# Stage boundaries by token tile: what a reordered normalisation and a new buffer layout do in a two-block transformer kernel

## The reference

```python
def rms_norm(x, g):
    xf = x.astype(jnp.float32)
    y = xf * lax.rsqrt(jnp.mean(xf * xf, -1, keepdims=True) + EPS)
    return (y * g.astype(jnp.float32)).astype(x.dtype)

for i in range(DEPTH):                       # DEPTH = 2
    a = rms_norm(h, norm_g[i, 0])
    a = mixer(a, ...)                        # i = 0: latent attention, i = 1: differential attention
    h = h + rms_norm(a, norm_g[i, 1])
    f = conv_ffn(rms_norm(h, norm_g[i, 2]), ffn_w_up[i], ffn_conv_w[i], ffn_conv_b[i], ffn_w_down[i])
    h = h + rms_norm(f, norm_g[i, 3])
# hybrid layer: rms_norm(h, g_mix) @ w_in, attention, then 32 experts, of which each token takes 2
```

## Time and profile before

| what | us |
|---|---|
| three runs | 1342.06, 1345.78, 1347.07; median 1345.78 |
| the profiled execution | 1344.84, of which the span from first to last instruction 1343.0 |
| TensorE busy | 1282.2 (95%) |
| GpSimd, ScalarE, VectorE busy | 573.2, 548.2, 509.6 |
| boundary `x1`: first idle-filling matmul to first product | 120.47 to 132.46 |
| boundary `x2` | 316.03 to 328.01 |
| boundary `x3` | 451.98 to 463.96 |
| boundary `x4` | 647.02 to 656.96 |

### The profile page before, as it was taken

The page is one execution under the profiler, slowest core; times in us unless marked ns, Lnnn a source line. Parts: engine busy times, 40 slices in busy tenths (PEclk is TensorE's granted clock), DMA queues, the critical chain, the costliest instruction groups (busy, mean ns, idle before and its releaser), DMA issues.

```text
span 1343.0 us, 20033 instructions
## 1 busy us (share of the span) xinstructions
PE 1282.2 (95%) x7959; PEld 953.8 (71%) x7959; DVE 509.6 (38%) x1303; ACT 548.2 (41%) x853; POOL 573.2 (43%) x136
## 2 busy tenths in 40 slices
PE   6998999999998899999999999999999999999996
PEld 6867999998986799999878888854444444454442
DVE  2434444445265454444657453421111111111112
ACT  4654555556477465555543664311111111111112
POOL 4722788885944188888567855200000000000001
PEclk9999999999999999999999999999999999999998
DMA  7731566664633276664446544889999999999994
GB/s 270 235 94 63 184 194 188 188 193 151 220 126 95 63 205 195 196 188 165 150 164 204 158 137 161 335 342 405 427 428 427 429 429 429 429 428 428 428 424 185
DMA packets 157078, 341.22 MB, mean 254 GB/s; under 512 B 8554, under 2 KB 119499, under 8 KB 144331
## 3 DMA queue, kind: packets, MB, share of 16 engines
q1 hardware_dynamic: 157002, 340.18, 68.2%
HBM read 339.10 MB, written 1.05 MB: 253 GB/s over the span
## 4 chain that ended last, share of the span: by engine, by line
PE 77%; DMA 11%; ACT 4%; DVE 4%; POOL 2%; issue 1%; SPq 0%; ACTq 0%; DVEq 0%
PE bank L683 16%; PE bank L685 15%; PE bank L684 15%; PE bank L1258 12%; DMA ring<-in_w 6%; PE bank L1286 6%; DMA xspare<-in_w 4%; PE bank L1201 3%; PE bank L782 2%; POOL parts L635 2%; PE bank L693 1%; PE bank L1231 1%; ACT parts L1330 1%; PE bank L1119 1%; PE bank L1135 1%
## 5 line engine op out<-in xcount | busy, mean ns | idle before, releaser
L635 POOL TENSOR_TENSOR parts<-raw,parts 128x2048 fp32r<-128x2048 f32 (+4 forms) x128 | 568.0, 4464 | 289.8 <-ACT parts L1330 289.8
L683 PE MATMUL bank<-xh,parts 128*128 128x256 f32 x1032 | 288.0, 279 | 5.8 <-POOL parts L635 3.8
L684 PE MATMUL bank<-xl,parts 128*128 128x256 f32 x1032 | 285.8, 277 | 0.0
L685 PE MATMUL bank<-xh,parts 128*128 128x256 f32 x1032 | 285.8, 277 | 0.0
L1330 ACT ACTIVATE parts<-raw 128x2048 fp32r<-128x2048 f32 (+4 forms) x128 | 236.0, 1852 | 23.4 <-PE bank L683 8.5
L1258 PE MATMUL bank<-ring,room 128*64 128x512 f32 x768 | 226.1, 594 | 7.2 <-DMA ring<-in_w 5.3
L658 POOL TENSOR_TENSOR xn<-h,gpost 128x512 f32<-128x512 f32 x4 | 4.9, 1268 | 474.6 <-DVE h L2283 474.6
L683 PEld LDWEIGHTS bank<-xh,parts 128*128 128x128 f32 x1032 | 193.8, 188 | 12.4 <-issue 4.7
L684 PEld LDWEIGHTS bank<-xl,parts 128*128 128x128 f32 x1032 | 194.0, 188 | 0.8
L685 PEld LDWEIGHTS bank<-xh,parts 128*128 128x128 f32 x1032 | 194.0, 188 | 0.0
L1258 PEld LDWEIGHTS bank<-ring,room 128*64 128x64 f32 x768 | 72.6, 137 | 111.7 <-issue 111.7
(11 more groups left out here) (256 smaller groups left out, 1858.5 us busy)
## 6 DMA issues: line engine op xcount, KB each, us to landing
ring<-in_w SPq DMA_DIRECT2D x67, 2048.0 KB, 22.6
raw<-in_ffn_w_up SPq DMA_DIRECT2D x88, 512.0 KB, 4.9
raw<-in_ffn_w_down SPq DMA_DIRECT2D x44, 512.0 KB, 3.9
room<-in_w SPq DMA_DIRECT2D x11, 2048.0 KB, 19.9
xspare<-in_w SPq DMA_DIRECT2D x11, 2048.0 KB, 25.6
raw<-in_w_in SPq DMA_DIRECT2D x40, 512.0 KB, 4.0
raw<-in_diff_w_qkv SPq DMA_DIRECT2D x24, 512.0 KB, 4.6
ring<-in_w SPq DMA_DIRECT2D x10, 1024.0 KB, 25.0
```

The source lines that it names most:

```text
L635: pool.tensor_tensor(low[:, p % PARTS, 0:n], raw[:, p % RING, 0:n], high[:, p % PARTS, 0:n], ALU.subtract).then_inc(low_ready, 1)
L683: first = pe.matmul(out_, a[0], b[0], start=start, stop=False)
L684: pe.matmul(out_, a[0], b[1], start=False, stop=False)
L685: return first, pe.matmul(out_, a[1], b[0], start=False, stop=stop)
```

## The change

**Steps 2 and 3 go by token tile.** `turned_over` replaces `post`: gains, sums, guess, root and residual of tile 0 are issued before tile 1's, each root as a chain of one-column operations (`half_of`, `root_of`) with a guess of its own. `h` of tile 0 is thus written before tile 1's gain. In a network's last `down`, TensorE now ends the two banks of tile 0 before it does tile 1's.

**Steps 4 and 5 in `x1` to `x3`.** The normalised `xn` is not written any more. For each tile, VectorE makes a diagonal matrix of the roots (`spread_roots`: identity times the root's column, [128 x 128] into `score`), and TensorE multiplies `h` by it (`h_transposed`), which turns and scales in one matmul. A bank now holds two whole feature tiles of [128 x 256], and so all four banks end with tile 1. The gain, which now lies along the partitions, is applied while copying out: `high_chunks` and `low_chunks`, eight operations of [128 x 256] on each engine, with a [128 x 1] column of `gcol` as scale.

**In `x4`** `h` itself is transposed as soon as each tile is there, and the gain is applied in the same way. The sum of squares, the guess and the roots come after.

**`k_tile`** waits bank by bank, at `k` = 0, 2, 4, 6, where there was one wait before the product and one at `k` = 4.

**Matmuls without use:** 23 for 32 in `x1` to `x3`; in `x4` 5, and 11 between the two tiles.

**Gains:** the four rows of gains come by small transfers into the rows that are transposed once in the first mixer, and VectorE copies 32 columns from there to `gcol`. SyncE's loads of `gpre` for these four boundaries are gone.

**Layout:** `xh`, `xl` (with `xspare`), `hh`, `hl`, `h`, `xn`, `room`, `gpre`, `gpost`, `score`, `selT` and `cs` now follow the ring in this order, the small buffers last. By the allocator each of the named ones lies 128 bytes past a multiple of 512, as the ring and `parts` do and did.

```diff
         ring = sb("ring", [P, 3 * RING, HALF])
+        with nc.sbuf_tensor("xh", [P, KT, S], F32R) as xh, nc.sbuf_tensor("xl", [P, KT, S], F32R) as xl:
+            pass
+        xspare = sb("xspare", [P, 2 * HALF])
+        hh, hl = sb("hh", [P, 4, S], F32R), sb("hl", [P, 4, S], F32R)
+        h = sb("h", [P, NT, D])
+        xn = sb("xn", [P, NT, D])
+        room = sb("room", [P, 11648])
+        gpre, gpost = sb("gpre", [P, D]), sb("gpost", [P, D])
+        score = sb("score", [P, NT, S])
+        selT = sb("selT", [P, 2, NT, P], F32R)
...
+            for x, src in enumerate((A["norm_g"][0, 2], A["norm_g"][1, 0], A["norm_g"][1, 2], A["g_mix_2"][0])):
+                rows_on(prow[1 + KT * x:1 + KT * x + KT, 4, :], src)
...
+            def h_transposed(name, site, scaled, between=0):
+                b = [begin(G[name] + q) for q in range(4)]
+                for t in range(NT):
+                    if t and between:
+                        keep_clock(between, bank[4])
+                    if scaled:
+                        pe.wait_ge(spread_ready, 2 * (site - 1) + t + 1)
+                    else:
+                        pe.wait_ge(h_ready, 2 * (site - 1) + t + 1)
+                    for k in range(KT):
+                        at = S * (k % 2) + P * t
+                        dst, src = b[k // 2][:, at:at + P], h[:, t, P * k:P * k + P]
+                        if scaled:
+                            ins = pe.matmul(dst, src, spread_r[:, t], start=True, stop=True)
+                        else:
+                            ins = pe.transpose(dst, src, ident)
+                        if t == 0 and k == 0:
+                            behind(ins)
+                        if t and k % 2:
+                            end(ins, G[name] + k // 2)
+                late.extend([(2 * q, G[name] + q) for q in range(4)])
...
-            WAIT = 32
+            WAIT = 23
             late = []
             def k_tile(k):
-                if k == 4:
-                    while late:
-                        moved(pe, late.pop(0))
+                while late and late[0][0] <= k:
+                    moved(pe, late.pop(0)[1])
...
-                    for x in range(2):
-                        pe.wait_ge(hid_ready, n + (n0 + 1 + x))
-                        for t in range(NT):
-                            for hf in range(2):
-                                first, ins = product(bank[4 + 2 * t + hf][:, :],
-                                                     [y[:, (j + x) % 4, t * P:t * P + P] for y in (hh, hl)],
-                                                     [y[:, x, 512 * hf:512 * hf + 512] for y in w],
-                                                     start and x == 0, stop and x == 1)
-                                behind(first)
-                                if stop and x == 1:
-                                    ins.then_inc(ffn_full, 1)
+                    each = [(x, t, hf) for x in range(2) for t in range(NT) for hf in range(2)]
+                    if stop:
+                        each = [(x, t, hf) for t in range(NT) for x in range(2) for hf in range(2)]
+                    for i, (x, t, hf) in enumerate(each):
+                        if not any(x == y for y, _, _ in each[:i]):
+                            pe.wait_ge(hid_ready, n + (n0 + 1 + x))
+                        first, ins = product(bank[4 + 2 * t + hf][:, :],
+                                             [y[:, (j + x) % 4, t * P:t * P + P] for y in (hh, hl)],
+                                             [y[:, x, 512 * hf:512 * hf + 512] for y in w],
+                                             start and x == 0, stop and x == 1)
+                        behind(first)
+                        if stop and x == 1:
...
+            keep_clock(WAIT // 4, bank[3])
+            h_transposed("x4", 4, False, WAIT // 2)
...
+            def high_chunks(name, site):
+                for k in range(KT):
+                    g = G[name] + k // 2
+                    full(act, g)
+                    act.activation(xh[:, k, :], bank[BANK[g]][:, S * (k % 2):S * (k % 2) + S], ACT.Copy,
+                                   scale=gain_of(site, k)).then_inc(x_high, 1)
...
-                    if n == 0:
+                    squares(st[:, 2 + n:3 + n], bank[b][:, :], view(6400 + 512 * n, 512), post_squares)
+                    if n % 2:
+                        t = n // 2
                         outs_done[0] += 1
-                    squares(st[:, 2 + n:3 + n], bank[b][:, :], view(6400 + 512 * n, 512), post_squares)
-                act.wait_ge(sums_ready, outs_done[0])
-                guess(st[:, 16:18], st[:, 18:20], D)
+                        act.wait_ge(sums_ready, outs_done[0])
+                        guess(st[:, 16 + t:17 + t], st[:, 18 + t:19 + t], D)
...
+            def low_chunks(name, site):
+                for k in range(KT):
+                    g = G[name] + k // 2
+                    x_parts[0] += 1
+                    dve.wait_ge(x_high, x_parts[0] + (1 - k % 2))
+                    ins = dve.scalar_tensor_tensor(xl[:, k, :], bank[BANK[g]][:, S * (k % 2):S * (k % 2) + S],
+                                                   gain_of(site, k), xh[:, k, :], ALU.mult, ALU.subtract)
+                    if k % 2:
+                        ins.then_inc(bank_moved[BANK[g]], 1)
...
+            def root_of(t, y):
+                guesses[0] += 1
+                dve.wait_ge(guessed, guesses[0])
+                dve.wait_ge(vec, steps[0])
+                a = st[:, 48 + t:49 + t]
+                link(dve.tensor_scalar(a, y, y, st[:, 32 + t:33 + t], ALU.mult, ALU.mult))
+                link(dve.tensor_scalar(y, a, 1.5, y, ALU.add, ALU.mult))
...
+            def turned_over(site, banks, ring_groups):
+                def gained_half(t, hf):
+                    b = banks[2 * t + hf]
+                    dve.wait_ge(post_squares, 4 * site + 2 * t + hf + 1)
+                    x = slice(512 * hf, 512 * hf + 512)
+                    ins = dve.tensor_tensor(xn[:, t, x], bank[b][:, :], gpost[:, x], ALU.mult)
                     ins.then_inc(bank_moved[b] if ring_groups else vec, 1)
-                if not ring_groups:
-                    steps[0] += 4
-                sums = st[:, 2:6].rearrange("p (t h) -> p t h", h=2)
-                dve.tensor_tensor(st[:, 18:20], sums[:, :, 0], sums[:, :, 1], ALU.add).then_inc(sums_ready, 1)
-                dve.wait_ge(sums_ready, site + 1)
-                refined(st[:, 16:18], st[:, 18:20])
-                for g in ring_groups or []:
-                    moved(dve, g)
-                for t in range(NT):
+                    if not ring_groups:
+                        steps[0] += 1
+                def summed(t):
+                    dve.wait_ge(post_squares, 4 * site + 2 * t + 2)
+                    dve.tensor_tensor(st[:, 18 + t:19 + t], st[:, 2 + 2 * t:3 + 2 * t], st[:, 3 + 2 * t:4 + 2 * t],
+                                      ALU.add).then_inc(sums_ready, 1)
+                    dve.wait_ge(sums_ready, 2 * site + t + 1)
+                    half_of(t, st[:, 18 + t:19 + t])
+                def residual(t):
+                    root_of(t, st[:, 16 + t:17 + t])
+                    for g in (ring_groups or [])[2 * t:2 * t + 2]:
+                        moved(dve, g)
                     dve.scalar_tensor_tensor(h[:, t, :], xn[:, t, :], st[:, 16 + t:17 + t], h[:, t, :],
                                              ALU.mult, ALU.add).then_inc(h_ready, 1)
+                dve.wait_ge(gpost_here, 16 * (site + 1))
+                gained_half(0, 0)
+                summed(0)
+                gained_half(0, 1)
+                residual(0)
+                gained_half(1, 0)
+                summed(1)
+                gained_half(1, 1)
+                residual(1)
+            def spread_roots(site):
+                for t in range(NT):
+                    dve.wait_ge(h_squares, 2 * site + t + 1)
+                    half_of(t, st[:, t:t + 1])
+                    root_of(t, st[:, 28 + t:29 + t])
+                    dve.tensor_scalar(spread_r[:, t], ident, st[:, 28 + t:29 + t], None, ALU.mult).then_inc(spread_ready, 1)
+            def x_transposed(name, site):
+                spread_roots(site)
+                low_chunks(name, site)
...
+            low_chunks("x4", 4)
+            scales(4)
...
```

110 lines of the change are left out of this document (45 added, 65 removed).

## The result

| | median us | range | runs |
|---|---|---|---|
| before | 1345.65 | 1342.06 to 1347.07 | 4 |
| changed | 1358.97 | 1357.83 to 1360.81 | 4 |

The ratio is 1.0093, with a 95% interval of [1.0064, 1.0121]. The forecast was 1335, its range ended at 1341.5, and rival (d), to which I gave 0.04, had put the time at 1355.

The account below looks back on a forecast made before the run. The front two thirds were taken as bound by TensorE and the four boundaries, the last third by a fixed-rate stream of expert weights. -7.5 - 3.0 + 0.4 = -10.1 us gave 1334.7, so 1335; range 1329 to 1341.5.

Parts of the forecast that it names:

- rival (d): TensorE's products: the new layout makes them slower, up to +21 us, less 10, time 1355; chance 0.04.
- Layout: Buffer addresses: no effect on TensorE's pace; ten expert loads into room lose 0.04 each, +0.4 us.
- the bound, 21: Products of lines 683 to 685: all 4680 going from one pace to the other, up to 21 us either way.
- Gain at `x2`: 2.5: Boundary x2, from T (first matmul without use) to the next product: 9.5 us in place of 12.0.
- GpSimd's hold on VectorE: Shared port: a diagonal could wait up to a piece's 4.6 us; GpSimd idle then, so six diagonals cost 0.28.
- Sum 0.15: VectorE's addition of a tile's sums of squares in the chain at x2, priced at 0.15 us.
- The pieces of GpSimd: Third pieces at x1 and x3 move along; later pieces at x2 and x4 are covered, by 1.0 us at the least.
- rival (a): Boundaries: GpSimd's pieces or the paced copies take half back, gain 6.5 us, time 1338.5; chance 0.12.
- Rival (b): Clock: with fewer useless matmuls it may fall to half at each boundary, +6.8 us, time 1341.5; chance 0.09.
- The sum of the turns: The four boundaries: -7.5 us for x1 to x3 together and -3.0 for x4.

Follow-up runs that it names:

- e2: The kernel before, with every buffer where the changed kernel has it and the old boundaries: 1363.88 us, ratio 1.0125 to before.
- e5: The changed kernel with the old buffer layout, and the one-column sum made as tensor_scalar in place of tensor_tensor: 1337.73 us, ratio 0.9935 to before.
- e14: The kernel of e5 with 32 useless matmuls in place of 23 at x1, x2 and x3: 1341.65 us, ratio 0.9964 to before.
- e12: The kernel of e5 with only hh and hl moved by 64 bytes, to the parts' place: 1342.97 us, ratio 0.9986 to before.

## Why the prediction was wrong

**The step that failed is "Layout": "So I take nothing for TensorE".** It is +18.0 by `e2`, alone more than all the rest. The rows in front of me were good: 256-column products had two paces at one address. I concluded that the address does not decide. What they show is that something else also decides. They bear on one difference of places, -64, and the change set another, 0, of which only line 712 said anything. That is a cost without a row, and the rule for those is to bound it from both sides: I worked out the bound, 21, and then left it out of the range. Rival (d) had the direction and the cause, a moved operand, but its 1355 is near the 1359 in part by luck. It sent all 4680 products from the faster of the two known paces to the slower, 4.5 ns each; measured are 5.6 ns at the mean of 3240 matmuls, to a third pace that no row of before has, and 1.4 ns less for those of 512 columns. Line 712, which I called no slower with equal places, is a 512-column matmul. Those are faster with equal places, by 1.2 to 2.3 ns, and it could not speak for the others: in the earlier trace rows, less the 0.39 us recorded for one alone, (7.44 - 0.39)/31 is 227.4 ns, against 229 for the products beside it.

**"Gain at `x2`: 2.5" failed too, by a price that the prediction quoted.** I weighed GpSimd's hold on VectorE for the six diagonals alone, and found GpSimd idle when they run. But the sum of tile 0 moves from T+1.6 to T-1.8, into GpSimd's last piece, which ends at T+0.2 to T+0.5. "Sum 0.15" was a duration with GpSimd idle. It took 2.02; in the profile of the change `x2` came out 4.1 above the forecast (13.55 for 9.5), of which 2.2 are the wait and 1.6 the clock behind it; `e5` gave back 1.6 of the 2.7 in the turns alone. At `x4` the same sum took 0.74, and the boundary 7.59 for 6.9; with the column it was 7.02.

**Right, with sizes.** `x1` and `x3`: 9.67 for 9.5. In steps, at `x1`, forecast and measured from T: h of tile 0 +1.0 and +0.9; h of tile 1 +4.4 and +4.1; TensorE's first tile +5.45 and +5.3; second diagonal +6.85 and +6.5; ScalarE's first copy +7.4 and +7.8; product +9.2 and +9.7. (The forecast's 6.57 for tile 1's root holds 0.1 more than its terms add up to.) VectorE's and ScalarE's new operations came as priced (lines: count, min/median/max ns):

```profile
L1905 DVE TENSOR_SCALAR score<-cs,st x6: 286/286/288, 125.1 to 463.9; 128x128 f32<-128x128 f32 x6
...
L1426 ACT ACTIVATE xh<-bank,gcol x32: 466/489/520, 128.1 to 666.1; 128x256 fp32r<-128x256 f32 x32
```

The low parts at `x1` (timeline of VectorE):

```profile
128.94 2.44 DVE L1828 SCALAR_TENSOR_TENSOR xl<-bank,gcol,xh 128x256 fp32r<-128x256 f32 x6 [2.16 <-ACT xh L1426]
```

Diagonals 0.29 for 0.28, copies 0.49 for 0.48, low parts (2.44 - 0.48)/5 = 0.39 apart for 0.38. TensorE's did not: a matmul with the diagonal was priced as a transpose, 0.12, and was recorded as two matmuls, 0.22 together; the sixteen took 3.81 for some 1.9. Most of that hides behind the chain of tile 1. What is left is that tile 0's eight end at some +7.1, behind the second diagonal, and that a bank takes twice as long: ScalarE's first copy comes 1.3 behind the second diagonal, for the 0.55 of the forecast, and eats what the steps before it had gained. The pieces of GpSimd did move along, with no new wait at `x2` or `x4`: rival (a) did not happen. Rival (b) did, in part: four half-clock stretches for two. I had argued that the gaps are no wider. The gap in question, at the third piece, was indeed as wide as before, and with 23 useless matmuls ahead of it the clock fell at 18 of 26 such gaps, with 32 at none of six.

**The sum of the turns.** The forecast for the turns without the layout was -10.5. The fixed kernel `e5` shows, against before and from the same stretches, -2.2, -1.35, -2.2 and -2.9 at the four boundaries, -8.7, and +1.6 in the second feed-forward stage, in which its clock fell for 3.4 us. Its 1337.7 is the best time of all, 0.65% under before.

**Open.** Why -64 has two paces, 113.6 and 117.7, and what picks one. It changes within a stage: the kernel before begins its first feed-forward stage at 117.8 and is at 113.5 from some 160 us on, and `e14` begins its second at about 114 and goes over to 117.8. `e5` and `e14` differ in nothing that the second feed-forward stage executes, and show one each; whether the pace differs between executions of one kernel can't be told from one profile each. At 4 ns by some 1000 matmuls a stage, that is about 4 us, as much as the runs of one kernel differ by, and about as much as `e5` is ahead of `e12` and `e14`. That two reads of one memory meet (the stream that moves and the weights being loaded) would fit a rule on differences, but no run shows it by itself. The Trainium skill, SBUF — State Buffer, section "Who interferes with whom", gives TensorE two read ports, one for the moving operand and one for the weight load, and calls them independent; in these runs the pace depends on where the two operands stand against each other, so for the time the measurement decides.

## What to carry to other kernels

When a change moves the buffers that TensorE reads, its pace has to be measured, since no row of before can give it: keep the old distances (modulo 512 bytes) between the moving and the stationary operands where they are good, and treat "aligned" as one more untried place. When a short VectorE instruction with two SBUF inputs moves earlier, look what GpSimd does at its new time, not at its old one; a one-column addition is free of it if one input is handed over as the scalar. And a bound that was worked out belongs in the range, whatever chance it is given.
